# A decoder layer with routed experts: in the expert loop, VectorE transposes the next rows first and computes the next gather's indices later

## The reference

```python
logits = h @ w_router + b_router
top_val, top_exp = lax.top_k(logits, TOP_K)          # TOP_K = 4
gate_w = jax.nn.softmax(top_val, axis=-1)
def expert_block(args):
    xb, e = args
    gt = jnp.minimum(xb @ w_gate[e] + b_gate[e], SWIGLU_LIMIT)                  # 7.0
    up = jnp.clip(xb @ w_up[e] + b_up[e], -SWIGLU_LIMIT, SWIGLU_LIMIT)
    return (gt * jax.nn.sigmoid(SWIGLU_ALPHA * gt) * (up + 1.0)) @ w_down[e] + b_down[e]
y = jax.ops.segment_sum(y_pad[dest] * sorted_w[:, None], sorted_tok, num_segments=T)
x = layer_norm(DEEPNORM_ALPHA * x + (1.0 + g2) * y, ln2_gain, ln2_bias)
```

## Time and profile before

| | |
|---|---|
| median of three runs | 1660.23 us |
| the profiled execution | 1664.65 us, span of its records 1662.5 us |
| PE busy | 1392.5 us (84%) |
| DVE busy | 801.4 us (48%) |
| ACT, POOL busy | 199.2 us (12%), 284.4 us (17%) |
| moved by DMA | 488.14 MB, 294 GB/s in the mean |
| gate/up matmuls (L1049) | 669.5 us busy, 171.2 us idle before them, 139.9 of it for the transfer of `in_w_up` |
| down matmuls (L1059) | 329.2 us busy, 4.6 us idle before them |

### The profile page before, as it was taken

One profiled execution on the slowest core, in us unless ns is written; L12 is line 12 of the kernel. 1 busy time (PEld: TensorE's weight loads), 2 busy tenths in 40 slices (PEclk: granted clock), 3 DMA queues, 4 the chain that ended last, 5 costly groups with the idle time before them and its releaser, 6 DMA issues. The chain is left out here.

```text
span 1662.5 us, 38826 instructions
## 1 busy us (share of the span) xinstructions
PE 1392.5 (84%) x13037; PEld 570.9 (34%) x13038; DVE 801.4 (48%) x2823; ACT 199.2 (12%) x522; POOL 284.4 (17%) x217
## 2 busy tenths in 40 slices
PE   6999988889949874778796997897999996969683
PEld 3444454454423321222231342242333331413121
DVE  1129675554885422334442554454455553525244
ACT  0011255550010000000000000000000000000002
POOL 0000000012531210111111221121122221212111
PEclk8999979989959996888987999898999997979786
DMA  9821066724176999999999889889989979496993
GB/s 343 213 76 51 1 219 219 245 92 177 53 295 246 405 410 411 407 411 406 406 358 414 305 311 406 311 314 400 405 310 406 357 263 377 137 408 219 405 410 142
DMA packets 161042, 488.14 MB, mean 294 GB/s; under 512 B 39792, under 2 KB 58284, under 8 KB 143597
## 3 DMA queue, kind: packets, MB, share of 16 engines
q1 hardware_dynamic: 144876, 470.84, 73.0%
q0 software_dynamic: 16128, 16.82, 5.0%
HBM read 474.40 MB, written 17.76 MB: 296 GB/s over the span
## 5 line engine op out<-in xcount | busy, mean ns | idle before, releaser
L1049 PE MATMUL banks<-arena,misc 128*32 128x512 f32 x5248 | 669.5, 640 | 171.2 <-DMA arena<-in_w_up 139.9
L1049 PEld LDWEIGHTS banks<-arena,misc 128*32 128x32 f32 x5248 | 164.1, 113 | 570.1 <-DMA arena<-in_w_up 312.7
L1059 PE MATMUL banks<-arena,master 128*32 128x256 f32 x5248 | 329.2, 393 | 4.6 <-DVE master L1613 2.1
L1795 DVE TENSOR_SCALAR cst<-banks 128x256 f32<-128x256 f32 x82 | 34.8, 424 | 423.9 <-PE banks L1049 421.1
L1059 PEld LDWEIGHTS banks<-arena,master 128*32 128x32 f32 x5248 | 168.1, 113 | 156.4 <-issue 71.1
L652 POOL DMA_INDIRECT misc<-moe_input,misc x84 | 88.3, 1051 | 723.1 <-DVE misc L1638 693.3
L668 POOL DMA_INDIRECT moe_output<-misc x82 | 130.2, 1587 | 228.4 <-issue 224.6
L1280 ACT ACTIVATE banks<-cst 128x256 f32<-128x256 f32 x82 | 31.8, 388 | 1078.4 <-DVE cst L1795 1078.4
L817 PE MATMUL banks<-arena 128*128 128x512 f32 x256 | 112.6, 595 | 0.0
L1618 DVE TENSOR_SCALAR master<-cbias 128x128 bf16<-128x128 f32 x340 | 94.9, 343 | 12.6 <-issue 6.0
L1657 DVE LOAD_MASK_SELECT banks<-master x84 | 1.2, 14 | 172.5 <-DMA master<-expert_bias 162.1
(11 more groups left out here) (309 smaller groups left out, 1112.0 us busy)
## 6 DMA issues: line engine op xcount, KB each, us to landing
arena<-in_w_gate SPq DMA_DIRECT2D x256, 512.0 KB, 12.4
arena<-in_w_up SPq DMA_DIRECT2D x256, 512.0 KB, 15.4
arena<-in_w_down SPq DMA_DIRECT2D x128, 1024.0 KB, 16.1
arena<-in_w_ada SPq DMA_DIRECT2D x12, 2048.0 KB, 13.1
arena<-in_x SPq DMA_DIRECT2D x2, 2048.0 KB, 8.6
arena<-in_w_in SPq DMA_DIRECT2D x2, 2048.0 KB, 9.8
master<-bias_by_distance SPq DMA_DIRECT2D x16, 256.0 KB, 4.5
arena<-in_w_in SPq DMA_DIRECT2D x8, 256.0 KB, 4.2
```

Of the source, the lines that this page charges most:

```text
L1049: last = nc.tensor.matmul(two(bank[2 * b][strip(j), :]), hTe[:, k, :], arena[:, 24 * b + 2 * k:24 * b + 2 * k + 2, quarter(j)], start=Fals ...
L1059: last = nc.tensor.matmul(bank[2 * b + 1][strip(j), 0:256], actT[:, q, c, :], DN(b, q, c)[:, quarter(j)], start=False, stop=(q == 3 and c ...
```

## The change

In `body`, the call of `rows_transposed` moves from behind the two clips to ahead of them, and `moved_on` and `slot_values` move from ahead of the product to behind `down_bias`. Nothing is added or taken away, and the other engines' programs are the same.

```diff
             def body(b, m, here, landed, bias_landed):
                 dve.wait_ge(s_a, m + 1)
+                rows_transposed(here)
                 dve.wait_ge(s_pr, m + 1)
                 nc.vector.tensor_scalar(gcl, bank[2 * b][:, 0:256], 7.0, None, ALU.min).then_inc(s_gdr, 1)
                 dve.wait_ge(s_act, m + 1)
                 nc.vector.tensor_scalar(ucl, bank[2 * b][:, 256:512], 7.0, -7.0, ALU.min, ALU.max).then_inc(s_urd, 1)
-                rows_transposed(here)
-                moved_on(m + 2, m + 2, m * 2 + 4, m + 1)
-                slot_values(m + 3, m * 2 + 5)
                 dve.wait_ge(s_gdr, m + 1)
                 dve.wait_ge(s_sig, m + 1)
                 nc.vector.tensor_tensor(gcl, sig, gcl, ALU.mult).then_inc(s_pr, 1)
...
                 nc.vector.scalar_tensor_tensor(gcl, ucl, 1.0, gcl, ALU.add, ALU.mult).then_inc(s_act, 1)
                 activations_transposed(m + 2, m + 1)
                 down_bias(b, bias_landed, m + 1)
+                moved_on(m + 2, m + 2, m * 2 + 4, m + 1)
+                slot_values(m + 3, m * 2 + 5)
                 one_hot(expert_of(ds(m + 3, 1)))
                 scatter_indices(m + 3, landed)
```

## The result

The changed kernel takes 1675.12 us (median of four runs, 1672.86 to 1678.97) against 1660.68 us: a ratio of 1.0085, with a 95% interval of 1.006 to 1.011. A second measurement of the same two kernels gave 1673.55 against 1661.73 us, 1.0069 (1.0054 to 1.0083). So the change costs 12 to 14 us. The direction and the mechanism are those of the forecast; its size, 5 us, was too small, and both measured times lie above the range of 1658 to 1672.5 us.

A forecast was written before the change was run, and what follows sets the result against it. Bound by the weight stream where items bring new experts, else by PE (10.65 us per item). Gather-cycle losses of 5.1 us plus 0.3 us tail made 5.4 us: 1665.6 us from 1660.23 (+0.33%), range 1658 to 1672.5.

The forecast's parts named there:

- The gains priced at nothing: Expert loop: row transpose 0.68 us earlier and activations about 0.5 us earlier gain nothing, since PE is still busy.
- the late DVE pays: Rival: where a bias transfer held DVE, PE starts 0.68 us sooner at eight places; -5.4 us, 1654.8 us; chance 0.09.
- The chain to the gather: From the row transpose's start through DVE's slot work to POOL's next gather: 5.25 us in the new order.
- The landing of 5.9 us: Time from a gather's start until its rows land beside a weight stream; bounded by 5.0 to 6.1 us.
- the stretches that count: Five stretches between expert loads that wait for PE, 923 to 1342 us; forecast loss 5.1 us together.
- the excess per item: Beside a weight stream the transpose-to-transpose cycle is 11.18 us against PE's 10.64: 0.54 us lost per item after slack.
- The slack of 0.92 us: How far into a PE-bound item the row transpose may start before PE waits: 0.92 us, used up after two items.
- At stretches at the stream's pace: nothing: Where each item brings a new expert (760 to 800 us), the weight stream sets the time; no loss.
- The point from which it decides: Gather cycle costs only above PE's item of 10.64 us; a landing of 5.0 us gives 10.28 and no loss.
- Only one buffer holds gathered rows: Reason given in the loop why a gather must land before the next row transpose; cycle 8.3 us before, 11.18 after.
- The descriptors: Rival: DVE's one-hot comparisons (1.1 us) shut out POOL's descriptor writing; cycle 12.3 us, +24 us, 1684; chance 0.08.
- The upper bound of 12.0 us: Whole kernel's loss with a landing of 6.1 and shuffle pitch of 0.59: cycle 11.55, 0.91 us per item.

The follow-up runs named there:

- both kernels whose gather starts later still: Changed kernel, slot work behind the one-hot work: 1706.51 us, 1.0263; earlier kernel, POOL's gather also waiting for the one-hot matrix: 1691.7 us, 1.0175.
- the kernel without the stream: Loop's weight transfers cut to 128 of 1024 columns: kernel before 1408.72 us, changed kernel 1409.59 us.

## Why the prediction was right in its way and wrong in its size

**The gains priced at nothing: right.** The earlier row transpose, the earlier activations and the iterations held by a bias transfer bring nothing; the half with the transpose alone measured 0.9995. The rival "the late DVE pays" is refuted.

**The chain to the gather: right.** 5.25 us forecast, 5.20 the median over the loop, 5.23 in the item shown. It is made up of small errors that cancelled: the shuffle's pitch is 0.33 us, not 0.42 (1238.73 to L1626 at 1239.06), the slot work 0.69, not 0.64 (1239.06 to 1239.75), and the hand-over from ACT 0.10, not 0.05 (1237.06 to 1237.16).

**The landing of 5.9 us: the term that was mis-sized.** I took it from one gather and a second one of the earlier trace rows, both in the middle of a running stream, and both issued earlier in the item (3.04 and 4.40 us) than the 5.23 us of the changed kernel. In the stretches that count, the row transpose follows the start of the 15 gathers I had counted by 6.22 us on average in the first profile of the change (from pairs as those shown above), so they land after 6.19 us. With 5.20 + 6.19 + 0.03 = 11.42 us the excess per item is 0.78 instead of 0.54 us: 3.6 us more in 15 items. The longest ones are gathers at the start of a stretch. In the kernel before, the gather of 965.71 had been issued 0.1 us ahead of a new expert's load (965.82) and its packets were through by 968.7, within 3.0 us; 2.2 us later in the item, the same gather falls in behind the load's first transfers (967.26 the load, 969.37 the gather, 7.26 us). I had moved the gather in time, but kept its landing.

**The gathers that POOL issues late: a term left out.** There are two, in both kernels. The one of the earlier trace rows was evidence for the landing, and I did not price its lateness. In the changed kernel the two start 6.13 and 6.58 us behind their row transpose (1072.23 to 1078.36, 1280.37 to 1286.95) instead of 5.20, 2.3 us together. With the 3.6 us of the landing and 0.1 us of slack in each of five stretches this makes 6.4 of the 6.7 us by which the five stretches exceed the forecast.

**The slack of 0.92 us: 0.8.** An item without a late gather shows it:

```profile
1422.84 1.93 PE L1059 MATMUL banks<-arena,master 128*32 128x256 f32 x32
1422.89 0.66 DVE L1607 STREAM_TRANSPOSE misc<-misc 128x256 f32<-128x256 f32 x1 [3.31 <-PE banks L1049]
...
1424.59 0.61 PE L1049 MATMUL banks<-arena,misc 128*32 128x512 f32 x4
```

The transpose with its wait for the gather starts 0.05 us behind PE's down matmuls, where the clip had started 0.05 us ahead of them (the clip at 1230.44 of the earlier trace rows came before those matmuls); the due time is 1424.59 - 0.23 - 0.66 = 1423.70, 0.81 us later.

**"At stretches at the stream's pace: nothing": right, but one stretch was missing.** At the full stream the loss comes back (items 35 to 36 give back 3.7 us of 8.8 in the first profile). Missing were the first items: the third gather is issued at 505.86 us, and PE waits for it.

```profile
505.86 1.07 POOL L652 DMA_INDIRECT misc<-moe_input,misc  x1 [9.49 <-DVE misc L1638]
...
512.92 0.63 DVE L1607 STREAM_TRANSPOSE misc<-misc 128x256 f32<-128x256 f32 x1 [5.25 <-DMA misc<-moe_input,misc]
...
513.80 5.36 PE L1049 MATMUL banks<-arena,misc 128*32 128x512 f32 x48 [1.61 <-DVE misc L1607]
```

This one could have been seen: in the kernel before, the row transposes of these items stand 10.49 to 10.73 us apart, PE's own pace, beside a stream that had begun. The 1.3 us of waiting for a gather in the earlier trace rows would not have told it. That wait is at the first row transpose of all, ahead of the loop, and the changed kernel has it as well:

```profile
490.06 0.64 DVE L1607 STREAM_TRANSPOSE misc<-misc 128x256 f32<-128x256 f32 x1 [1.30 <-DMA misc<-moe_input,misc]
```

What the first items cost is uncertain: items 0 to 26 take 2.6 and 3.1 us more in the two profiles of the change, but only 1.0 more in both kernels whose gather starts later still.

**The point from which it decides: right.** The knee between 4.2 and 4.8 us fits 10.64 - 6.2 = 4.4 us, with the mean landing.

**"Only one buffer holds gathered rows": not the reason.** The gather waits for L1638 in 81 of 84 cases (824.0 us), not for the transpose that empties the buffer. A second buffer alone would not open the ring, since the indices still hang behind the transpose in DVE's order; this was not tried.

**The descriptors: no block, but a trace of something.** L652 lasts 1113 ns in the mean instead of 1051, in the kernel without the stream too (1.11). It is not the comparisons (L1618) that do it. With the slot work ahead of the down bias the gather runs beside them and takes 1.05 us in the mean. In the changed kernel it also runs beside a small copy (L1620) and a cast (L1644), and there all three are longer: the copy takes 0.41 us instead of 0.17, the cast 0.34 instead of 0.14. Both end at 1241.98, just ahead of the gather's instruction (1242.01). With half the rows that instruction takes 1.05 us, and the copy 0.34 and the cast 0.27.

```profile
1240.90 1.11 POOL L652 DMA_INDIRECT misc<-moe_input,misc  x1 [7.82 <-DVE misc L1638]
...
1241.57 0.41 DVE L1620 COPY cbias<-cbias 128x12 bf16 x1
1241.64 0.34 DVE L1644 CAST misc<-misc 128x1 uint32<-128x1 f32 x1
```

The same in the kernel with the slot work ahead of the down bias, where the gather's instruction ends at 1248.98, as they begin:

```profile
1247.93 1.05 POOL L652 DMA_INDIRECT misc<-moe_input,misc  x1 [6.30 <-DVE misc L1638]
...
1248.94 0.17 DVE L1620 COPY cbias<-cbias 128x12 bf16 x1
1249.01 0.14 DVE L1644 CAST misc<-misc 128x1 uint32<-128x1 f32 x1
```

The Trainium skill (SBUF — State Buffer, "Who interferes with whom") says that DVE and GpSimd share one pair of ports; whether the longer copy, cast and gather are that, no run here shows. A block of the gather for the length of the comparisons, as in that rival, is refuted. The 0.06 us of the gather are part of the landings measured above, and the run without a stream bounds the whole effect at about a microsecond.

**Bounds.** The upper bound of 12.0 us held for the second measurement by a hair (+11.8) and not for the first (+14.4). It was worked out with the longest landing that one item showed, not with the spread over items.

## What to carry to other kernels

When an instruction that starts a transfer is moved, look for the ring that it closes: from the consumer of one transfer over the issue of the next to the next consumer, and compare its length with the period of the engine that bounds. Below it the move is free, above it each item pays the excess, and here half a microsecond on either side decided. The landing time of a small gather is to be taken from many gathers at the instant at which they will be issued, not from the one that is at hand.

A sum of waits has a place. Before the 1.3 us of a table are read, either as "hidden everywhere" or as "no slack left", one look at where they stand settles it: here it was ahead of the loop, where the change does nothing.

## What the runs showed of the hardware

Most of a small gather's landing beside a full weight stream is neither its issue nor its data. These are the DMA queues (packets, MB, share of 16 engines) in the changed kernel, first in 1242 to 1245 us, then in 1245 to 1246.6 us; the gather's issue ended at 1242.0.

```profile
q1 hardware_dynamic: 348, 1.27, 103.4%
...
q1 hardware_dynamic: 135, 0.50, 80.0%
q0 software_dynamic: 48, 0.13, 22.0%
```

For 3 us not one packet of POOL's queue moves; then the whole gather goes through in 1.6 us at most. This fits that half the rows shortened the landing by only 0.4 us (from the gather's start to a row transpose that waits for it in the loop, 6.19 us in the mean of 45 pairs in the changed kernel, 5.81 in 41 with half the rows). Without a stream the silence is shorter. In the kernel before, the gather of 1416.94 moves no packet until 1418.6, and all 48 of them by 1419.6. So from the start of the issue to the first packet it is about 1.7 us there, and at least 4.1 us beside the stream. What the queue waits for in that time, no view here shows.
